# One TensorE-bound hybrid block: how the conditioning weights and x arrive, and how the gated norm is built

## The reference

```python
ada = silu(c) @ w_ada + b_ada                     # w_ada is 1024 x 3072
shift, scale, gate = split(ada, 3)
h = rmsnorm(x, norm_w) * (1 + scale) + shift      # x itself is needed again for the residual
proj = h @ w_in                                   # z, xbc, dt, q, k, v, z_att, f, g
...
y_ssm = rmsnorm(y * silu(z), ssm_norm_w)          # y from the state-space scan over xbc
```

## Time and profile before

| what | value |
|---|---|
| median of three runs | 2137.48 us |
| the profiled execution | 2143.57 us, its span 2142.0 us |
| granted TensorE clock, mean | 0.974 |
| TensorE matmul, busy | 2021.1 us (94%) |
| VectorE, busy | 1000.9 us (47%) |
| ScalarE, busy | 775.2 us (36%) |
| GpSimd, busy | 163.4 us (8%) |
| DMA | 166.28 MB |

### The profile page before, as it was taken

The page is one execution under the profiler, slowest core; times in us unless marked ns, Lnnn a source line. Parts: engine busy times, 40 slices in busy tenths (PEclk is TensorE's granted clock), DMA queues, the critical chain, the costliest instruction groups (busy, mean ns, idle before and its releaser), DMA issues. The chain is left out here.

```text
span 2142.0 us, 27056 instructions
## 1 busy us (share of the span) xinstructions
PE 2021.1 (94%) x9946; PEld 1611.5 (75%) x9946; DVE 1000.9 (47%) x1210; ACT 775.2 (36%) x1130; POOL 163.4 (8%) x314
## 2 busy tenths in 40 slices
PE   6899999998999999999999999699999999999897
PEld 3677778776887888878787888478777777777786
DVE  4576545455223333343333344684333342543865
ACT  4423323244214444343443332341433343532422
POOL 0000111000100000000000100022000001111100
PEclk8899999999999999999999999899999999999998
DMA  7431655443521111111102533223111111110302
GB/s 276 168 71 40 109 108 98 99 139 98 161 83 30 39 39 39 49 29 39 49 29 78 167 114 93 98 85 113 35 40 29 32 49 30 49 39 17 125 28 89
DMA packets 165314, 166.28 MB, mean 78 GB/s; under 512 B 11402, under 2 KB 143938, under 8 KB 163970
## 3 DMA queue, kind: packets, MB, share of 16 engines
q1 hardware_dynamic: 151746, 116.11, 17.2%
q0 software_dynamic: 13504, 49.29, 9.7%
HBM read 132.22 MB, written 33.16 MB: 77 GB/s over the span
## 5 line engine op out<-in xcount | busy, mean ns | idle before, releaser
L288 PE MATMUL acc<-ha_hi,w_hi 128*128 128x512 f32 x1152 | 471.2, 409 | 4.2 <-ACT stash L301 2.9
L288 PE MATMUL acc<-ha_hi,w_lo 128*128 128x512 f32 x1152 | 453.0, 393 | 0.0
L288 PE MATMUL acc<-ha_lo,w_hi 128*128 128x512 f32 x1152 | 451.5, 392 | 0.0
L288 PEld LDWEIGHTS acc<-ha_hi,w_hi 128*128 128x128 f32 x1152 | 218.5, 190 | 52.7 <-issue 9.7
L288 PEld LDWEIGHTS acc<-ha_hi,w_lo 128*128 128x128 f32 x1152 | 217.5, 189 | 48.1
L288 PEld LDWEIGHTS acc<-ha_lo,w_hi 128*128 128x128 f32 x1152 | 218.4, 190 | 41.8
L257 DVE TENSOR_TENSOR w_lo<-w_raw,w_hi 128x1024 fp32r<-128x1024 f32 x128 | 159.4, 1245 | 139.6 <-ACT w_hi L253 136.9
L271 PE MATMUL acc<-ha_hi,w_hi 128*128 128x512 f32 x592 | 187.7, 399 | 27.8 <-DVE ha_lo L1740 13.5
L271 PE MATMUL acc<-ha_lo,w_hi 128*128 128x512 f32 x592 | 185.1, 394 | 0.0
L271 PE MATMUL acc<-ha_hi,w_lo 128*128 128x512 f32 x592 | 184.9, 394 | 0.0
L271 PEld LDWEIGHTS acc<-ha_hi,w_hi 128*128 128x128 f32 x592 | 111.2, 191 | 58.6 <-issue 15.7
(11 more groups left out here) (418 smaller groups left out, 2918.6 us busy)
## 6 DMA issues: line engine op xcount, KB each, us to landing
w_raw<-in_w_in SPq DMA_DIRECT2D x99, 512.0 KB, 3.7
w_ada<-in_w_ada SPq DMA_DIRECT2D x8, 1024.0 KB, 11.8
acs_bc<-acs_scr POOLq DMA_DIRECT2D x8, 1024.0 KB, 15.8
w_raw<-in_w_out SPq DMA_DIRECT2D x11, 512.0 KB, 3.7
x_tok<-in_x SPq DMA_DIRECT2D x8, 512.0 KB, 7.4
xt_scr<-xt SPq DMA_DIRECT2D x1, 4096.0 KB, 24.0
w_ada_g<-in_w_ada SPq DMA_DIRECT2D x8, 512.0 KB, 9.5
z_scr<-stash SPq DMA_DIRECT2D x8, 512.0 KB, 10.8
```

The source lines that it names most:

```text
L288: mm = pe.matmul(acc[:, 0, half * HALF:(half + 1) * HALF], w[:, n % 2, k, :], x[:, k, half * HALF:(half + 1) * HALF], start=(k == 0 and i ...
```

## The change

In stage 0 the shift and scale columns of `w_ada` get a place of their own for each of the eight slices (`w_shift`, `w_scale`), so no load waits for a slot. There are sixteen loads of 512 KB, in the order of `ADA_ORDER`; a pair of them waits for what its semaphore counted before: the first four pairs for a pair of x tiles, the other four for the pair eight loads earlier. The 14 small vectors are issued by ScalarE, ahead of its first wait, and are turned first. The squares come in pairs with a root after each pair. The scaling writes to `x_norm`, so x stays as it is: normed turns come first, and raw turns afterwards, one ahead of each shift product. Which engine copies what is dealt out anew: of the normed halves ScalarE copies 5 and VectorE 11, of the raw halves ScalarE 12 and VectorE 4 (after the scale slices 3 to 6). The column sums come before the last shift product; the shift row is copied and spread in two halves. The save of `xt` has to wait for the last raw copy. The gate part of `w_ada` waits for the last shift product, since it lies over `w_shift`.

In stage 2 the read of z applies Silu. In stage 3 the Silu of z, `yw` and the pairwise sums are gone: VectorE multiplies `xbc` by z one tile ahead, ScalarE makes `ya_hi` with the norm's weight as its scale, VectorE makes `ya_lo` with the weight in the same instruction, and the squares go to `y_sq` and are all summed in `xbc[:, 0]`. The place of `split_hi`, `split_lo` and `gate` between the tiles changes. In stage 4 one pair of ones matmuls is left.

```diff
-        def read_half(act, n, half, m, dst, adv=0):
+        def read_half(act, n, half, m, dst, adv=0, func=ACT.Copy):
...
-            return act.activation(dst[:, s], acc[:, 0, s], ACT.Copy).then_inc(fill_free, 1)
+            return act.activation(dst[:, s], acc[:, 0, s], func).then_inc(fill_free, 1)
...
-        ADA_RING = 4
-        w_ada = Region(at_ha, at_ha + big)("w_ada", [P, ADA_RING, 2 * D])
+        x_norm = Region(at_ya, at_ya + big)("x_norm", [P, NT, D])
+        w_scale = Region(at_ha, at_ha + big)("w_scale", [P, KT, D])
+        w_shift = Region(at_ya + big, at_ya + 2 * big)("w_shift", [P, KT, D])
...
+        SCALE, SHIFT = 0, 1
+        ADA_ORDER = ([(SCALE, 0), (SCALE, 1)] + [e for k in range(KT - 2) for e in ((SHIFT, k), (SCALE, k + 2))]
+                     + [(SHIFT, KT - 2), (SHIFT, KT - 1)])
...
-            def load_ada(k):
-                if k >= ADA_RING and k % 2 == 0:
-                    sp.wait_ge(slice_scaled, k - ADA_RING + 2)
-                    sp.wait_ge(shift_added, k - ADA_RING + 2)
-                if k % 2 == 0:
-                    sp.wait_ge(pair_loaded[k // 2], 32)
-                sp.dma_start(w_ada[:, k % ADA_RING, :], wa[:, k, 0:2 * D]).then_inc(pair_loaded[k // 2], 16)
...
+            def load_ada(j):
+                part, k = ADA_ORDER[j]
+                if j % 2 == 0:
+                    sp.wait_ge(pair_loaded[j // 2 % 4], 32 * (j // 8 + 1))
...
-            for k in range(ADA_RING, KT):
-                load_ada(k)
+            for j in range(8, 2 * KT):
+                load_ada(j)
             load_w(sp, N_XBC, cols(w_in, XBC_OFF))
-            sp.wait_ge(xt_act, NT)
-            sp.wait_ge(xt_dve, NT)
+            sp.wait_ge(xt_act, XT_ACT)
+            sp.wait_ge(xt_dve, XT_DVE)
             sp.dma_start(xt_scr, xt[:, :, :]).then_inc(xt_saved, 16)
             load_w(sp, N_XBC + 1, cols(w_in, XBC_OFF + P))
+            sp.wait_ge(shift_added, KT)
...
+            for dst, src in vec_sources():
+                act.dma_start(dst, src).then_inc(vec_loaded, 16)
             act.wait_ge(consts, 1)
...
+            for q in range(NT // 2):
+                square(2 * q)
+                square(2 * q + 1)
+                roots(q)
+                if q:
+                    copy_xn(2 * q - 2)
...
+            copy_xn(NT - 2)
+            copy_xn(NT - 1)
+            for i in range(NT):
+                for g in range(1 if i < XT_DVE else 2):
+                    copy_xt(i, g)
             act.wait_ge(col_loaded, 16 * 8)
...
+            def add_shift(k):
+                ada_landed(pe, SHIFT, k)
+                for h in range(2):
+                    mm = pe.matmul(work[SHIFT_AT[h], h, :], silu_c[:, k:k + 1], w_shift[:, k, h * HALF:(h + 1) * HALF],
+                                   start=(k == 0), stop=(k == KT - 1))
+                mm.then_inc(shift_added, 1)
...
+            for k in range(KT - 1):
+                turn_raw(k)
+                add_shift(k)
+            turn_raw(KT - 1)
+            pe.wait_ge(dve_steps, 1)
+            sum_columns(pe, scale_sum, work[:, 2, KT:2 * KT])
+            add_shift(KT - 1)
...
-                    read_half(act, N_Z + 2 * c + i, half, 2 * c + i, stash[:, i, :])
+                    read_half(act, N_Z + 2 * c + i, half, 2 * c + i, stash[:, i, :], func=ACT.Copy if i else ACT.Silu)
...
+            def tile(f):
+                act.wait_ge(yz_done, f + 3)
+                act.activation(ya_hi[:, f, :], xbc[:, f, :], ACT.Copy, scale=dcol(vec1, VEC1, "ssm_norm_w", f)).then_inc(x_hi_done, 1)
+                if f >= 2:
+                    act.wait_ge(sq_added, f - 1)
+                act.activation(y_sq[:, f % 2, :], xbc[:, f, :], ACT.Square).then_inc(Norm.squared, 1)
...
+            for f in range(3):
+                tile(f)
+            gate(0, 0)
+            split_hi(act, N_GATT + 2)
+            tile(3)
+            gate(0, 1)
+            tile(4)
+            tile(5)
+            gate(1, 0)
+            split_hi(act, N_GATT + 3)
+            tile(6)
+            gate(1, 1)
+            tile(7)
+            gate(2, 0)
+            split_hi(act, N_MIX1)
+            gate(2, 1)
+            gate(3, 0)
             split_hi(act, N_MIX1 + 1)
+            gate(3, 1)
...
+            gated(0)
+            for f in range(KT):
+                if f in (4, 7):
+                    split_lo(dve, N_GATT + (2 if f == 4 else 3))
+                if f + 1 < KT:
+                    gated(f + 1)
+                low(f)
+                if f >= 2:
+                    add_square(f - 1)
+            add_square(KT - 1)
+            split_lo(dve, N_MIX1)
             split_lo(dve, N_MIX1 + 1)
...
-            for f in range(0, KT, 2):
-                for h in range(2):
-                    mm = pe.matmul(work[:, h, :], ones[:, :], xbc[:, f, h * HALF:(h + 1) * HALF],
-                                   start=(f == 0), stop=(f == KT - 2))
-                mm.then_inc(norm4.summed, 2)
+            for h in range(2):
+                mm = pe.matmul(work[:, h, :], ones[:, :], xbc[:, 0, h * HALF:(h + 1) * HALF], start=True, stop=True)
+            mm.then_inc(norm4.summed, KT)
```

More of the change, by code:

```diff
@@ L390, in build @@
         x_tok = ar("x_tok", [P, NT, D])
-        x_sq0 = ar("x_sq0", [P, 2, D])
         scale_sum = ar("scale_sum", [P, D])
@@ L572, in pe_0 @@
[L572 to L575, removed]
                 turn_normed(i)
-            pe.wait_ge(xt_act, NT)
-            pe.wait_ge(xt_dve, NT)
             pe.wait_ge(silu_c_done, 1)
-            for k in range(KT):
-                pe.wait_ge(pair_loaded[k // 2], 64)
-                for h in range(2):
-                    mm = pe.matmul(acc[0:1, 1, h * HALF:(h + 1) * HALF], silu_c[:, k:k + 1],
-                                   w_ada[:, k % ADA_RING, h * HALF:(h + 1) * HALF], start=(k == 0), stop=(k == KT - 1))
-                mm.then_inc(shift_added, 1)
@@ L586, in pe_0 @@
-            pe.wait_ge(xn_act, NT)
-            pe.wait_ge(xn_dve, NT)
-            pe.wait_ge(silu_c_done, 2)
-            for m in range(KT):
-                pe.matmul(work[:, 2, m:m + 1], shift_row[0:1, m * P:(m + 1) * P], ones[0:1, 0:1], start=True, stop=True)
-            pe.wait_ge(dve_steps, 1)
-            sum_columns(pe, scale_sum, work[:, 2, KT:2 * KT]).then_inc(ada_mul, 1)
+            pe.wait_ge(xn_act, XN_ACT)
+            pe.wait_ge(xn_dve, XN_DVE)
+            for k in range(KT - 1):
+                turn_raw(k)
+                add_shift(k)
@@ new lines, in pe_0 @@
+            turn_raw(KT - 1)
+            pe.wait_ge(dve_steps, 1)
+            sum_columns(pe, scale_sum, work[:, 2, KT:2 * KT])
+            add_shift(KT - 1)
+            for m in range(KT):
+                h = m // 4
+                if m % 4 == 0:
+                    pe.wait_ge(silu_c_done, 2 + h)
+                mm = pe.matmul(work[:, 2, m:m + 1], shift_row[0:1, m * P:(m + 1) * P], ones[0:1, 0:1],
+                               start=True, stop=True)
+            mm.then_inc(ada_mul, 1)
@@ new lines, in tile, with gate @@
+            def tile(f):
[4 more added lines that the diff above has]
+                act.activation(y_sq[:, f % 2, :], xbc[:, f, :], ACT.Square).then_inc(Norm.squared, 1)
+            def gate(i, half):
+                n = N_GATT + i
+                projected(act, n)
+                act.wait_ge(ga_saved, 32 * i + 16 * half + 16)
+                e = act.activation(ga_half[:, :], acc[:, n % 2, half * HALF:(half + 1) * HALF], ACT.Copy)
+                if half:
+                    e.then_inc(acc_free[n % 2], 1)
+                act.drain().then_inc(ga_ready, 1)
@@ L1166, in dve_3, with gated, low @@
             dve.drain().then_inc(yz_done, 2)
-            for f in range(KT):
-                b = f % 2
-                if f and b == 0:
-                    split_lo(dve, N_GATT + f // 2 + 1)
-                dve.wait_ge(z_silued, f + 1)
-                dve.scalar_tensor_tensor(yw[:, b, :], xbc[:, f, :], dcol(vec1, VEC1, "ssm_norm_w", f), silu_z[:, b, :],
-                                         ALU.mult, ALU.mult)
-                dve.tensor_tensor(xbc[:, f, :], xbc[:, f, :], silu_z[:, b, :], ALU.mult)
+            def gated(f):
+                dve.wait_ge(z_loaded[f % 2], 16 * (f // 2) + 16)
+                dve.tensor_tensor(xbc[:, f, :], xbc[:, f, :], silu_z[:, f % 2, :], ALU.mult)
                 dve.drain().then_inc(yz_done, 1)
+            def low(f):
                 dve.wait_ge(x_hi_done, SPLITS[3] + f + 1)
```

198 lines of the change are left out of this document (90 added, 108 removed).

## The result

| | before | after |
|---|---|---|
| median | 2137.05 us (2135.18 to 2138.18, 4 runs) | 2125.03 us (2123.87 to 2127.09, 4 runs) |
| span of the profiled execution | 2142.0 us | 2125.5 us |
| TensorE busy | 2021.1 us | 2004.8 us |
| granted clock, mean | 0.974 | 0.978 |

The ratio is 0.994, with a 95% interval of 0.9928 to 0.9952: the change takes 12.0 us off the median. The two profiled executions differ by 16.5 us, because before's was itself 6.5 us above its median and after's 2.1.

The account below looks back on a forecast made before the run. TensorE, busy for nearly all of the span, was taken as the bound, so savings count only where it stops or runs slowly. +1.1 + 1.3 − 8.0 − 4.9 = −10.5 us, from 2137.48 to 2127.0 us; range 2124 to 2131.

Parts of the forecast that it names:

- Landings: Stage 0: late `w_ada` loads, issued 5.7 us earlier, still stand behind `dskip`; no gain in the last landing, bounds 0 and 5.7.
- Rival A: Start: `dskip` does not hold the queue, late loads land 5.7 us earlier, `ada` about 5 us sooner; 2122 us, chance 0.2.
- Vector loads and turns: Stage 0: moving vector loads to ScalarE's queue costs nothing; turns end at 43.4 at worst, ahead of the 45.9 landing.
- The start's chain: Stage 0: raw turns between shift products lie on TensorE's path; `ada` at 66.2 against 65.13, +1.1 us.
- Silu: Scan's z reads: added table loads are covered in seven chunks, exposed in the first; stop 2.95 to 4.2, +1.3 us.
- Rival D: Scan: table loads are not covered, TensorE waits for the z read in each chunk; 19.2 us cost, 2144.9, chance 0.04.
- The norm: Gated norm: gate tiles' pieces come earlier, TensorE goes on without a stop ahead of `N_MIX1` at full clock, -8.0 us.
- Ones matmuls: After the gated norm: twelve of sixteen ones matmuls go, at 0.41 us each, -4.9 us.
- The three later terms: Scan, gated norm and ones matmuls: +1.3 us for Silu, -8.0 for the norm, -4.9 for the ones matmuls.

## Why the prediction was right, step by step

The forecast was 2127.0 us, the median 2125.03, inside the range; its mechanism held, with terms that were off in both directions.

1. *Landings.* Right in kind: `dskip` holds the queue, and the run without it in the way settles it. The first late pair was in at 43.8, not 45.9, and the last by about 51, not 53.4 (261 GB/s from 48 to 50 us, 39 from 50 to 52). Most of these 2 us lie in the reference: the late group that I took from 48.40 started at 45.5 to 46.1 in the other three executions of that code. Rival A, that `dskip` holds nothing, is out.
2. *Vector loads and turns*: nothing, as said; TensorE was idle from 33.8 until 43.77.
3. *The start's chain.* The structure was right, its terms were not. From the landing to the end of the last shift product it took 12.4 us and not 17.5, above all because a shift step is 1.03 us and not 1.76: I took that from before's L583, whose matmuls all go to one output row. The tail took 4.6 us and not 2.8: I had put the weight's high part at nothing and the spreading products at the full clock. With the landing 2.1 us earlier `ada` came at 60.77 and not at 66.2. That my +1.1 us is nearer to the medians (0, between −1.7 and +2.1 by the interval) than the −4.4 that the traces give is luck: my end of the chain was 5.4 us too late, and the 65.13 against which I reckoned was itself a late one.
4. *Silu.* Only the first chunk is exposed: stop 4.37 for my 4.2. The scan's cost is 2.1 us in the trace, since the low clock behind the stop lasts longer; I had 1.3 as value, with nothing for the clock, and 3.7 as bound. Rival D is out. By the Trainium skill's 2.66 us a switch (ScalarE: Activation LUTs, "What ACT_TABLE_LOAD costs") the stop would have grown by 2.7; it grew by 1.42, one load and no drain.
5. *The norm.* −7.97 us in the trace for −8.0. The reason given was half of it: the bank's late read ended the stop, but the run with the early read alone shows that the tiles' rate has to rise as well. Step 5 had both, and put the stop down to the read. No run had the faster tiles without the earlier read.
6. *Ones matmuls.* −5.2 us in the traces, 3.9 in medians and 4.9 in ratios, for −4.9.

The three later terms add up to −11.0 in the traces and −10.3 in the medians of the run that has them alone, for my −11.6. What is left open is whether the start's part gains a microsecond or loses one; eleven runs of each kernel don't tell. Why the clock falls early in some executions of before's stage 0 was not tried.

## What to carry to other kernels

A load of single floats held up everything behind it in its queue here: put such a load last, and only then judge whether buffers' reuse matters, since either cure alone showed little of the 11 us that the pair gave. An engine's late read that ends a stop need not be its cause: ask what is late next, and move the work that covers it in the same step. Before a trace's time for an event is used as a reference, look at the granted clock of the stretch before it, and if the execution was far from the median, at a second one.

## What the hardware showed that I had not expected

- One code had `ada` at 59.3 and 59.8 us in the executions whose granted clock was 1.00 over the first 20 us, and at 62.8 and 65.1 in those with 0.92 and 0.91.
- Four one-row float32 matmuls, two to output partition 0 and two to 64, take 1.03 us, against 1.88 with all to the same partition.
- A stop of 2.62 us was followed by 7.09 us for 32 matmuls that take 3.79 at the full clock: here the low clock cost more than the stop.
